# FFN output product: stationary tiles 16 bytes further each, and two of three products with their columns backwards

## The chip, the cores and the metric

The kernel runs on one core of a Trainium2 chip. The metric is the device time of one execution in microseconds. The time before is the median of three runs.

## The reference

Two transformer blocks on one sequence of 256 positions and a width of 2048, all in float32. What bears on the change is the feed-forward part of the first block:

```python
D_FF = -(-8 * D_MODEL // (3 * 256)) * 256          # 5632

def swiglu(x, w_in, w_out):
    g, u = jnp.split(x @ w_in, 2, axis=-1)
    return (jax.nn.silu(g) * u) @ w_out

# in first_block
y = swiglu(x, w_ffn_in[l], w_ffn_out[l])            # [256, 2048] @ [2048, 11264], [256, 5632] @ [5632, 2048]
x = layer_norm(ALPHA * x + y, ln_g[l, 2], ln_b[l, 2])
```

Ahead of it stand a mixer of two attentions and a memory attention; behind it the second block. They are not changed.

## The kernel before

All dense products of the kernel go through one scheme. A weight matrix comes in groups: two tiles of 128 rows and 512 columns (GK = 2, NB = 512), 512 KB, loaded by SyncE into one of four slots of `stage` (L328). ScalarE copies a group into `w_hi` in TensorE's reduced float32 format, fp32r (L1241), and VectorE puts what is left, `stage - w_hi`, into `w_lo` (L1705). The activations are split the same way. A float32 product is then three fp32r products: hi with upper weights, hi with the rest, lo with upper weights. `upper(slot)` and `rest(slot)` give the slot's part of `w_hi` and `w_lo`; from four groups ahead of the second block on, two extra slots (`more_stage`, `more_hi`, `more_lo`) take part for twelve groups.

The queue of TensorE is written out by hand. `weights(kts, hi, lo)` walks the groups of one block of 512 output columns; `group` waits for `lo_done`, then calls `half_group` for both halves r of the 256 rows. A half group is six matmuls into the PSUM bank ACC + r: for each of the two tiles t the three products above, with the activations' 128 x 128 tile as the stationary operand and 512 weight columns as the moving one. Each matmul comes with a weight load of its own. The loop in question is

```python
for k, (x, w) in enumerate(((hi, upper), (hi, rest), (lo, upper))):
    ins = mm(ps[:, ACC + r, 0:n], x[:, kt + t, rows], w(slot)[:, t, 0:n],
             start=first and t == 0 and k == 0, stop=last and t == GK - 1 and k == 2)
```

The feed-forward part works in three parts of 4, 4 and 3 blocks of 512 hidden units (FFN_PARTS). In each, `silu(g) * u` is computed block by block, transposed on TensorE (L732), and written by ScalarE into `ff_h` (L1297) and by VectorE into `ff_l` (L1754), two tiles of 128 x 256 at a time. Then the output product follows: four blocks of 512 columns with 16 (in the last part 12) tiles each, `weights(kts=4 * nf, hi=ff_h, lo=ff_l)`. Its `last_tile_at` waits for the last transposed tiles only ahead of group 2 (nf - 1). Over the three parts these are 44 x 4 x 2 = 352 triples of matmuls.

`ff_h` and `ff_l` are tensors of [128, 16, 256] in fp32r: per partition 16 tiles of 1024 bytes, one behind the other, then those of `ff_l`. Their place is shared in time with others: `more_stage` begins 32 KB behind the start of `ff_h`, which is where `ff_l` ends. A tile `align` of [128, 88] keeps the large tensors at their distance from the start of the memory. Other products use the same line with other activations, above all `x_hl` of [128, 16, 2, 256], whose hi and lo tiles alternate. `heads_block` (L707, L710) is the other way round: weights are stationary, activations move, with 512 and 256 columns in turn. The forget gate's product (L1133) has a stationary operand of 8 columns.

Of the kernel before, what the change touches and what calls it, by code (L numbers as in the profile page):

```python
# [22 lines left out]
F32R = mybir.dt.float32r  # L23
# [5 lines left out]
P = 128  # L29
S = 256  # L30
# [124 lines left out]
def some(value):  # L155

    return not isinstance(value, int) or value > 0


def two_blocks(nc, a, out, per):  # L160

    ctx = ExitStack()
    with ctx:
# [5 lines left out]
        def sem(name):  # L169
            if name not in sems:  # L170
                sems[name] = ctx.enter_context(nc.semaphore("s_" + name))
            return sems[name]
# [46 lines left out]
        def shared(*shapes):  # L219

            with ExitStack() as own:
                return [own.enter_context(nc.sbuf_tensor("b_" + n, s, t)) for n, s, t in shapes]
# [38 lines left out]
            ("kmem_t", [P, H_MEM, S], F32), ("vmem", [P, R, H_MEM * HD], F32))  # L261
        (qmem_t, om_h, om_l) = shared(
            ("qmem_t", [P, H_MEM, S], F32), ("om_h", [P, H_MEM, S], F32R), ("om_l", [P, H_MEM, S], F32R))
        (ff_h, ff_l) = shared(("ff_h", [P, 4 * 4, S], F32R), ("ff_l", [P, 4 * 4, S], F32R))
        (_, more_stage, more_hi, more_lo) = shared(
            ("pad_more", [P, 32 * S], F32), ("more_stage", [P, MORE, GK, NB], F32),
            ("more_hi", [P, MORE, GK, NB], F32R), ("more_lo", [P, MORE, GK, NB], F32R))
# [7 lines left out]
        ps = ctx.enter_context(nc.psum_tensor("b_ps", [P, 8, NB], F32))  # L275
        ACC, TP, SC, AUX, PT, OT = 0, 2, 4, 5, 6, 7
# [359 lines left out]
        def _(pe):  # L636

            c = Counts("pe", per)
            mm, T = nc.tensor.matmul, nc.tensor.transpose

            def group(kt, first, last, hi, lo, n=NB):

                slot, _ = slot_of(c.base.get("g", 0) + c.local.get("g", 0))
                pe.wait_ge(sem("lo_done"), c.next("lo_done"))
                for r in range(R):
                    half_group(slot, r, kt, first, last, hi, lo, n)
                c.next("g")

            def half_group(slot, r, kt, first, last, hi, lo, n=NB):

                if first and some(c.value(f"tile_out{r}")):
                    pe.wait_ge(sem(f"tile_out{r}"), c.value(f"tile_out{r}"))
                for t in range(GK):
                    rows = slice(r * P, (r + 1) * P)
                    for k, (x, w) in enumerate(((hi, upper), (hi, rest), (lo, upper))):
                        ins = mm(ps[:, ACC + r, 0:n], x[:, kt + t, rows], w(slot)[:, t, 0:n],  # L656
                                 start=first and t == 0 and k == 0, stop=last and t == GK - 1 and k == 2)
                if r == 1:
                    ins.then_inc(sem("w_used"), 1)
                elif last:  # L660
                    ins.then_inc(sem("tile0_done"), 1)

            def by_halves(n, kt, first, last, hi, lo, ready=None):

                slots = [slot_of(c.value("g") + i)[0] for i in range(n)]
                for r in range(R):
                    for i in range(n):
                        if ready:
                            ready(r, i)
                        if r == 0:  # L670
                            pe.wait_ge(sem("lo_done"), c.next("lo_done"))
                        half_group(slots[i], r, kt + i * GK, first and i == 0, last and i == n - 1, hi, lo)
                c.next("g", n)
# [410 lines left out]
            for kt in range(2):  # L1084
                pe.wait_ge(sem(f"tile_out{kt}"), c.value(f"tile_out{kt}"))
                for h in range(H_MEM):
                    if kt == 0:
                        pe.wait_ge(sem("pt_ready"), c.next("pt_ready"))
                    ins = mm(mem_out[h], vmem[:, kt, h * HD:(h + 1) * HD],
                             mem_pt[h][:, kt * S:(kt + 1) * S], start=kt == 0, stop=kt == 1)  # L1090
# [1411 lines left out]
def lay_out(nc, shapes, per):  # L2502
    a = {k: nc.dram_tensor("in_" + k, list(s), F32, kind="ExternalInput").ap() for k, s in shapes.items()}
    out = nc.dram_tensor("out", [S, D], F32, kind="ExternalOutput").ap()
    two_blocks(nc, a, out, per)
# [16 lines left out]
```

## Time and profile before

| | |
|---|---|
| median of three runs | 2231.52 us (2231.26 to 2232.51) |
| profiled execution, its own time | 2231.99 us |
| its span | 2230.4 us |
| TensorE busy | 2220.3 us |
| VectorE busy | 1304.6 us |
| ScalarE busy | 1053.9 us |
| GpSimd busy | 178.5 us |
| bytes read | 417.98 MB, 188 GB/s over the span |
| granted TensorE clock | full |

The span reaches from the first to the last instruction of the program; the execution's own time holds 1.6 us more. Busy times count the time in which at least one instruction of the engine is under way. Matmuls overlap each other in the records, so their single durations say little of the rate.

### The profile page before, as it was taken

The numbers are of one execution on the slowest core, as the hardware profiler recorded it, in microseconds if no ns is written. First come the engines' busy times: TensorE is split into PE (matmuls) and PEld (weight loads), VectorE is DVE, ScalarE is ACT, GpSimd is POOL, SyncE is SP. The second block draws the span as 40 slices with busy tenths as digits, with TensorE's granted clock in tenths as the row PEclk, the third lists the DMA queues.
The fourth block names the chain that finished last, engine by engine and source line by source line (L and its number), as shares of the span: only waits on it lengthen the run. The fifth ranks groups of instructions, "written<-read, shape, count | busy, mean of one in ns | idle before, by whom it ended". The sixth has DMA issues, their size and how long they took to land.

```text
span 2230.4 us, 29901 instructions
## 1 busy us (share of the span) xinstructions
PE 2220.3 (100%) x10457; PEld 1850.8 (83%) x10457; DVE 1304.6 (58%) x1589; ACT 1053.9 (47%) x1283; POOL 178.5 (8%) x187
## 2 busy tenths in 40 slices
PE   9999999999999999999999999999999999999999
PEld 8888888888888888888888888888888888888887
DVE  5556655666667754454545445566656655655674
ACT  4444445555444544443444334446445444545643
POOL 1000000001304220000000000003000000200020
PEclk9999999999999999999999999999999999999999
DMA  7755654656856466656665565654566656665554
GB/s 233 230 173 166 191 160 147 192 165 219 263 174 213 134 202 197 202 198 193 191 190 187 191 196 181 197 199 151 170 189 198 206 177 186 207 189 176 167 189 166
DMA packets 216873, 421.33 MB, mean 189 GB/s; under 512 B 15400, under 2 KB 19536, under 8 KB 215120
## 3 DMA queue, kind: packets, MB, share of 16 engines
q1 hardware_dynamic: 212928, 401.79, 57.0%
q0 software_dynamic: 3584, 17.83, 2.4%
q8 instruction: 57, 0.93, 0.2%
q10 hardware_dynamic: 272, 0.52, 0.1%
q14 instruction: 32, 0.26, 0.0%
HBM read 417.98 MB, written 2.11 MB: 188 GB/s over the span
## 4 chain that ended last, share of the span: by engine, by line
PE 98%; POOL 1%; DVE 1%; ACT 0%; DMA 0%; issue 0%; ACTq 0%; DVEq 0%; SPq 0%; POOLq 0%
PE b_ps L656 82%; PE b_ps L707 7%; PE b_ps L710 3%; PE b_ps L749 1%; PE b_ps L832 1%; PE b_ps L732 1%; PE b_ps L847 1%; POOL b_x_res L554 0%; PE b_ps L841 0%; POOL b_x_res L556 0%; PE b_ps L932 0%; PE b_ps L901 0%; PE b_ps L848 0%; DMA b_gate_a<-in_x 0%; DVE b_w_lo L1705 0%; PE b_ps L1133 0%
## 5 line engine op out<-in xcount | busy, mean ns | idle before, releaser
L656 PE MATMUL b_ps<-b_w_hi,b_x_hl 128*128 128x512 f32 (+1 forms) x4144 | 1312.7, 392 | 1.2 <-DVE b_x_hl L1780 1.1
L1705 DVE TENSOR_TENSOR b_w_lo<-b_stage,b_w_hi 128x1024 fp32r<-128x1024 f32 (+1 forms) x756 | 932.8, 1253 | 577.0 <-ACT b_w_hi L1241 573.8
L1241 ACT ACTIVATE b_w_hi<-b_stage 128x1024 fp32r<-128x1024 f32 (+1 forms) x758 | 790.3, 1054 | 677.3 <-PE b_ps L656 590.3
L656 PEld LDWEIGHTS b_ps<-b_w_hi,b_x_hl 128*128 128x128 f32 x4144 | 777.1, 188 | 159.2 <-DVE b_x_hl L1780 1.3
L656 PE MATMUL b_ps<-b_w_lo,b_x_hl 128*128 128x512 f32 (+1 forms) x2072 | 804.4, 388 | 0.0
L656 PEld LDWEIGHTS b_ps<-b_w_lo,b_x_hl 128*128 128x128 f32 x2072 | 389.5, 188 | 76.9
L707 PE MATMUL b_ps<-b_x_hl,b_w_hi 128*128 128x512 f32 x576 | 205.8, 402 | 0.2 <-DVE b_w_lo L1705 0.2
L710 PE MATMUL b_ps<-b_x_hl,b_w_lo 128*128 128x256 f32 x568 | 159.3, 281 | 0.0
L656 PE MATMUL b_ps<-b_w_hi,b_ff_h 128*128 128x512 f32 x344 | 134.1, 390 | 0.0
L656 PE MATMUL b_ps<-b_w_hi,b_ff_l 128*128 128x512 f32 x344 | 133.9, 389 | 0.0
L656 PE MATMUL b_ps<-b_w_lo,b_ff_h 128*128 128x512 f32 x344 | 133.9, 389 | 0.0
L707 PEld LDWEIGHTS b_ps<-b_x_hl,b_w_hi 128*128 128x128 f32 x576 | 108.7, 189 | 28.8 <-issue 3.2
L710 PEld LDWEIGHTS b_ps<-b_x_hl,b_w_lo 128*128 128x128 f32 x568 | 107.3, 189 | 0.0
L656 PEld LDWEIGHTS b_ps<-b_w_hi,b_ff_l 128*128 128x128 f32 x344 | 64.6, 188 | 13.5
L656 PEld LDWEIGHTS b_ps<-b_w_hi,b_ff_h 128*128 128x128 f32 x344 | 64.6, 188 | 13.4
L656 PEld LDWEIGHTS b_ps<-b_w_lo,b_ff_h 128*128 128x128 f32 x344 | 64.6, 188 | 13.2
L554 POOL TENSOR_TENSOR b_x_res<-b_x_res,b_vec_a 128x512 f32<-128x512 f32 x16 | 28.1, 1758 | 568.0 <-ACT b_x_res L1326 557.2
L1857 DVE SCALAR_TENSOR_TENSOR b_x_res<-b_x_res,b_ps 128x512 f32<-128x512 f32 (+1 forms) x48 | 33.0, 687 | 47.6 <-PE b_ps L656 47.1
L1373 ACT ACTIVATE b_logits<-b_logits,b_nmax 128x128 f32<-128x128 f32 (+1 forms) x48 | 21.5, 448 | 79.8 <-DVE b_nmax L1806 79.8
L656 PE MATMUL b_ps<-b_w_hi,b_oh 128*128 128x512 f32 x136 | 53.7, 395 | 0.0
L656 PE MATMUL b_ps<-b_w_hi,b_ol 128*128 128x512 f32 x136 | 53.0, 390 | 0.0
L656 PE MATMUL b_ps<-b_w_lo,b_oh 128*128 128x512 f32 x136 | 53.0, 389 | 0.0
(328 smaller groups left out, 1536.9 us busy)
## 6 DMA issues: line engine op xcount, KB each, us to landing
b_stage<-in_w_in SPq DMA_DIRECT2D x333, 512.0 KB, 4.1
b_stage<-in_w_ffn_in SPq DMA_DIRECT2D x176, 512.0 KB, 4.5
b_stage<-in_w_ffn_out SPq DMA_DIRECT2D x86, 512.0 KB, 4.0
b_stage<-in_w_out SPq DMA_DIRECT2D x64, 512.0 KB, 4.1
b_stage<-in_w_up SPq DMA_DIRECT2D x24, 512.0 KB, 4.0
b_stage<-in_w_o_dsa SPq DMA_DIRECT2D x16, 512.0 KB, 4.5
b_stage<-in_w_o_moba SPq DMA_DIRECT2D x16, 512.0 KB, 4.1
b_stage<-in_w_kv_mem SPq DMA_DIRECT2D x16, 512.0 KB, 3.6
```

The lines of the kernel that those rows point to most:

```text
L554: pool.tensor_tensor(x, x, vec_a[:, cols], ALU.mult).then_inc(sem("pool_step"), 1)
L656: ins = mm(ps[:, ACC + r, 0:n], x[:, kt + t, rows], w(slot)[:, t, 0:n], start=first and t == 0 and k == 0, stop=last and t == GK - 1 and k ...
L707: mm(ps[:, bank, :], upper(slot)[:, t, cols], flat(hl[:, j * GK + t, :, :]), start=j == 0 and t == 0, stop=False)
L710: ins = mm(ps[:, bank, 0:S], rest(slot)[:, t, cols], hl[:, j * GK + t, 0, :], start=False, stop=last and t == GK - 1)
L732: ins = T(ps[:, TP + j // 2, (j % 2) * S + r * P:(j % 2) * S + (r + 1) * P], nat[:, r, j * P:(j + 1) * P], ident[:, :])
L749: ins = T(ps[:, TP + t % 2, kk * S + r * P:kk * S + (r + 1) * P], src[:, r, (2 * t + kk) * P:(2 * t + kk + 1) * P], ident[:, :])
L832: ins = mm(ps[:, SC, lo:hi], q[:, t * P:(t + 1) * P], keys(hi - lo), start=k == 0, stop=k == len(pairs) - 1)
L847: mm(ps[:, bank, col:col + S], v0, probs_t[:, 0:S], start=True, stop=False)
L1241: act.activation(upper(slot)[:, :, 0:n], landing(slot)[:, :, 0:n], ACT.Copy)\
L1373: ins = act.activation(logits[:, 0, lo:hi], logits[:, 0, lo:hi], ACT.Exp, bias=nmax[:, t:t + 1], accum_out=rsum[:, t:t + 1])
L1705: dve.tensor_tensor(rest(slot)[:, :, 0:n], landing(slot)[:, :, 0:n], upper(slot)[:, :, 0:n].bitcast(F32), ALU.subtract).then_inc(sem("lo_d ...
L1857: dve.scalar_tensor_tensor(out=x, in0=x, scalar=alpha, in1=ps[:, ACC + r, :], op0=ALU.mult, op1=ALU.add).then_inc(sem(f"tile_out{r}"), 1)
```

## The change

The rows of `ff_h` and `ff_l` become four elements longer, 260 instead of 256. A tile keeps its 256 elements, and tile k of each tensor starts 16k bytes further than before; `ff_l` as a whole starts 256 bytes further. In the output product the two products with the upper weights (k = 0 and k = 2) read their 512 moving columns from the last to the first and write the result's columns in the same order, so each value lands where it did. The product with the rest of the weights (k = 1) stays forward. All other products are as before.

```diff
-        (ff_h, ff_l) = shared(("ff_h", [P, 4 * 4, S], F32R), ("ff_l", [P, 4 * 4, S], F32R))
+        (ff_rows, fl_rows) = shared(("ff_h", [P, 4 * 4, S + 4], F32R), ("ff_l", [P, 4 * 4, S + 4], F32R))
+        ff_h, ff_l = ff_rows[:, :, 0:S], fl_rows[:, :, 0:S]
@@
                     for k, (x, w) in enumerate(((hi, upper), (hi, rest), (lo, upper))):
-                        ins = mm(ps[:, ACC + r, 0:n], x[:, kt + t, rows], w(slot)[:, t, 0:n],
+                        to, by = ps[:, ACC + r, 0:n], w(slot)[:, t, 0:n]
+                        if hi is ff_h and k != 1:
+                            to, by = to[:, ::-1], by[:, ::-1]
+                        ins = mm(to, x[:, kt + t, rows], by,
                                  start=first and t == 0 and k == 0, stop=last and t == GK - 1 and k == 2)
```

## Rows read from the trace of the kernel before

**Rows 1.** The page: busy us (share of the span) and instructions; the chain by engine and line.
```profile
PE 2220.3 (100%) x10457; PEld 1850.8 (83%) x10457; DVE 1304.6 (58%) x1589; ACT 1053.9 (47%) x1283; POOL 178.5 (8%) x187
...
PE 98%; POOL 1%; DVE 1%; ACT 0%; DMA 0%; issue 0%; ACTq 0%; DVEq 0%; SPq 0%; POOLq 0%
PE b_ps L656 82%; PE b_ps L707 7%; PE b_ps L710 3%; PE b_ps L749 1%; PE b_ps L832 1%; PE b_ps L732 1%; PE b_ps L847 1%; POOL b_x_res L554 0%; PE b_ps L841 0%; POOL b_x_res L556 0%; PE b_ps L932 0%; PE b_ps L901 0%; PE b_ps L848 0%; DMA b_gate_a<-in_x 0%; DVE b_w_lo L1705 0%; PE b_ps L1133 0%
```

**Rows 2.** Busy time by stretch: the one with the output products.
```profile
core 0: us, PE busy (x) PEld busy (x) DVE busy (x) ACT busy (x) POOL busy (x), PEclk, DMA share, GB/s
...
949.00:1502.00 553.00, 553.00 (x2477) 458.56 (x2476) 286.35 (x272) 229.12 (x235) 1.26 (x2) 1.00 0.60 194
```

**Rows 3.** Instructions on the upper weights, by tile: duration ns min/median/max, first and last start.
```profile
L656 PE MATMUL b_ps<-b_w_hi,b_ff_h x344: 389/389/476, 950.0 to 1500.7; 128*128 128x512 f32 x172
...
L656 PE MATMUL b_ps<-b_more_hi,b_ff_h x8: 389/389/390, 1490.5 to 1497.9; 128*128 128x512 f32 x8
```

**Rows 4.** The chain in two output stretches, in order of time: start us, us, what.
```profile
952.92 0.87 PE b_ps L732 x8
953.79 130.58 PE b_ps L656 x576
...
1438.89 62.62 PE b_ps L656 x276
```

**Rows 5.** Timeline, 1000.5 to 1001.5 us: start us, us, engine, line, out<-in.
```profile
1000.57 0.39 PE L656 MATMUL b_ps<-b_w_hi,b_ff_h 128*128 128x512 f32 x1
1000.57 0.19 PEld L656 LDWEIGHTS b_ps<-b_w_lo,b_ff_h 128*128 128x128 f32 x1
1000.79 0.39 PE L656 MATMUL b_ps<-b_w_lo,b_ff_h 128*128 128x512 f32 x1
1000.79 0.19 PEld L656 LDWEIGHTS b_ps<-b_w_hi,b_ff_l 128*128 128x128 f32 x1
1001.02 0.39 PE L656 MATMUL b_ps<-b_w_hi,b_ff_l 128*128 128x512 f32 x1
...
1001.25 0.39 PE L656 MATMUL b_ps<-b_w_hi,b_ff_h 128*128 128x512 f32 x1
```

**Rows 6.** The chain at 36 us: L656 with 336 columns.
```profile
35.81 14.73 PE b_ps L656 x96
```

**Rows 7.** Instructions on ff_h and ff_l, by tile: their writers.
```profile
L1297 ACT ACTIVATE b_ff_h<-b_ps x22: 591/596/599, 820.4 to 1439.2; 128x512 f32 x16, 128x512 fp32r<-128x512 f32 x6
...
L1754 DVE TENSOR_TENSOR b_ff_l<-b_ps,b_ff_h x22: 680/686/692, 821.2 to 1440.0; 128x512 f32 x16, 128x512 fp32r<-128x512 f32 x6
```

**Rows 8.** The chain at the forget gate's product; its weight loads, by tile.
```profile
1530.92 3.21 PE b_ps L1133 x28
...
L1133 PEld LDWEIGHTS b_ps<-b_x_hl,b_wf x32: 87/88/88, 1530.1 to 1533.7; 128*8 128x8 f32 x32
```

**Rows 9.** Timeline of L707 and L710, three pairs at 77 us and three at 84 us.
```profile
77.23 0.40 PE L707 MATMUL b_ps<-b_x_hl,b_w_hi 128*128 128x512 f32 x1
77.46 0.28 PE L710 MATMUL b_ps<-b_x_hl,b_w_lo 128*128 128x256 f32 x1
77.58 0.40 PE L707 MATMUL b_ps<-b_x_hl,b_w_hi 128*128 128x512 f32 x1
77.82 0.28 PE L710 MATMUL b_ps<-b_x_hl,b_w_lo 128*128 128x256 f32 x1
...
78.29 0.40 PE L707 MATMUL b_ps<-b_x_hl,b_w_hi 128*128 128x512 f32 x1
...
83.98 0.39 PE L707 MATMUL b_ps<-b_x_hl,b_w_hi 128*128 128x512 f32 x1
84.21 0.28 PE L710 MATMUL b_ps<-b_x_hl,b_w_lo 128*128 128x256 f32 x1
...
85.02 0.39 PE L707 MATMUL b_ps<-b_x_hl,b_w_hi 128*128 128x512 f32 x1
```

**Rows 10.** The chain at 511 us: plain float32 products, 256 and 128 columns.
```profile
510.82 0.43 PE b_ps L847 x2
511.25 0.22 PE b_ps L848 x2
```

## The prediction

> **What bounds the kernel.** I read the page first: busy time, the forty slices, then the chain that ended last. TensorE is busy for 2220.3 of the 2230.4 us and the chain lies on it for 98% [rows 1]; the line of the change, L656, holds 82% of the chain. The granted clock is full in all slices. Then I cut the span at the products that change. They lie between 949 and 1502 us; in that stretch VectorE works 286 and ScalarE 229 of 553 us, and the DMA engines move 194 GB/s at a share of 0.60 [rows 2]. So in this stretch nothing but TensorE sets the time, and what the change costs or gives per matmul reaches the end of the kernel undiluted.
>
> A matmul's own duration (389 ns, [rows 3]) is useless here, since the matmuls are pipelined: it is the step from one start to the next that counts. The chain gives it best. 576 matmuls of L656 in 130.58 us are 226.7 ns each, and 276 in 62.62 us are 226.9 ns [rows 4]. Three forms of L656 stand in one group of six (w_hi with ff_h, w_lo with ff_h, w_hi with ff_l), and the timeline shows no difference between them: 0.22 or 0.23 us from start to start for all [rows 5].
>
> What is this step made of? The same line with 336 columns takes 14.73 us for 96 matmuls, 153.4 ns [rows 6]. From 336 to 512 columns 73.3 ns are added for 176 columns, which is 0.416 ns a column: one column per cycle of the 2.4 GHz clock. 512 columns are then 213.3 ns, and a pause of 13.4 ns is left at every matmul. Only two things can move: the 0.416 ns, if backward columns run at another rate, and the 13.4 ns, if the position of the stationary tile or the direction of the columns has a part in it.
>
> **The parts of the change.** No instruction is added or removed: the matmuls keep their number, order, banks and semaphores. The counts are 344 + 8 of each of the three forms [rows 3]: 1056 matmuls read a moved stationary tile, and the two forms with the upper weights, 704, run backwards.
>
> *The wider rows of ff_h and ff_l.* ScalarE and VectorE write two tiles at a time with a gap of 16 bytes instead of 512 elements in one piece, 22 times each, 596 and 686 ns [rows 7]. Even 0.1 us more for each of the 44 would be 4.4 us of two engines with some 590 us idle between them over the stretch (553 - 286 and 553 - 229); TensorE asks for the last tiles only after 2(nf - 1) groups, six groups of twelve matmuls or 16 us later in the first two parts. I put it at 0. ff_l now reaches 496 bytes into the first extra staging slot, but only with its sixteenth tile, which the third part (twelve tiles) does not use, and only in the third part is that slot filled. No wait: 0.
>
> *The moved tile as a source of weights.* The weight load takes 188 ns and starts together with the matmul before it [rows 5], so it ends 39 ns ahead of its use. A few nanoseconds more for a shifted start are hidden; were they over 39 ns, they would show in full. What is not hidden is what the load does to the columns that stream beside it. The nearest rows speak on both sides. With stationary tiles of 8 columns, 256 moving columns take 3.21 us for 28, 114.6 ns, so the pause is 114.6 - 106.7 = 8.0 ns [rows 8]: at most 13.4 - 8.0 = 5.4 ns seem to belong to the length of the weight load. And in the head projections, which alternate 512 and 256 columns, the same two lines take 1.06 us for three pairs at 77 us and 1.04 us at 84 us [rows 9], that is 353 against 347 ns a pair, in one and the same block, before and after a few transposes that stand between. Tensors and banks are the same, so I read that difference as one of phase between loads and columns, not of address; single steps there read 0.22 to 0.24 us. So a pause can change with how loads and columns meet, by 3 ns a matmul on the mean and some 10 ns in single ones.
>
> Nothing in the trace shows an operand off its grid: everywhere the step is 226.7 to 226.9 ns, with x_hl, whose tiles stand 2 KB apart, as with ff_h, whose tiles stand 1 KB apart. So I bound the price. Upwards: 10 ns on all 1056 is +10.6 us. Downwards: 5.4 ns on 704 is -3.8 us, on 1056 -5.7 us; the whole pause gone from the 704 backward ones is 704 x 13.4 = -9.4 us, from all 1056 -14.2 us. Nearest is the value that two layouts already share: 0. The Trainium skill, SBUF — State Buffer, "Who interferes with whom", says that TensorE has independent read ports for the moving operand and the weights and waits on nobody. By that rule the term is 0 as well, and both savings above are excluded; the row does not go as far, since it shows a pause without saying what it is.
>
> *The backward columns.* Moving operand and result both run from column 511 to 0, so both are still contiguous. Lower bound of the price: 0 per column. Upper bound: two cycles a column, as the rows with plain float32 operands show (eight 128-column transposes in 0.87 us, 109 ns each, 0.85 ns a column, [rows 4]; two 256-column products in 0.43 us, 0.84 ns a column, [rows 10]). That would be 704 x 213.3 = +150 us. I take 0: a walk of step minus one touches each place once and its neighbour next, as the forward one does, and no row shows a reason for a second cycle.
>
> *The turns.* In a triple the first product ends at result column 0 and the second begins there; the second ends at 511 and the third begins there. Before, each result column rested for a whole matmul between two additions. If an addition still under way held up the next one, it could only do so at the turn, two in each triple, 704 in all. The pause of 13.4 ns already lies between them. Bounds: 0 and, say, a second pause, 704 x 13.4 = +9.4 us. I take 0.
>
> **Sum.** 0 + 0 + 0 + 0. The profiled execution took 1.6 us more than its span, 2231.99 us, and stands 0.5 us above the median of 2231.52. I keep the median: 2231.5 us. What a measurement of this kernel can tell from no change is about 0.2%, 4.5 us, or 6.3 ns on each of the 704 matmuls.
>
> **Rivals.**
>
> *The pause shrinks by more than 0.2% of the time (0.31).* The weight load and the columns hinder each other in the memory they share, and a shifted tile read beside backward columns avoids it. For it: there is a pause at all; it is 5.4 ns shorter with small weights [rows 8]; it varies with phase [rows 9]. Against it: it is the same in x_hl and ff_h, and plain float32 products, whose columns come at half the rate, are not quite comparable. Time: from 2231.5 - 5.7 = 2225.8 to 2231.5 - 9.4 = 2222.1 us, at most 2217.3. It decides from 4.3 ns on all 1056 steps or 6.3 ns on the 704.
>
> *The pause grows by more than 0.2% of the time (0.18).* The tiles leave a grid on which every product of the kernel lies; or the turn waits. Place: the 1056 or the 704 steps of L656 with ff_h and ff_l; price 3 to 13 ns each; +3 to +11 us, up to 2242.5 us. It decides from 4.3 ns on all 1056, or 6.3 ns on 704. For it: the spread of [rows 9] goes upwards from 346.7 ns as easily as down. Against it: it is an effect of order, and the order of L656 has shown one value over thousands of steps.
>
> *The columns at half rate (0.11).* If the result's columns are joined in pairs before they are written, and only upwards, each takes two cycles: 2231.5 + 150 = 2382 us. Against it: the pair of columns lies in the same place either way. The Trainium skill, Advanced Engine Details and Errata, "PSUM Cachelines", says that any non-contiguous pattern slows matmuls significantly, with 8 bytes as the unit; it does not say whether backwards counts as contiguous. No row here shows a backward pattern.
>
> *No effect (0.40)* is the forecast: pause and column rate stay, within 4.5 us either way. Small shifts of the pause (a mean of 1 to 4 ns) belong to it; its own range is 2228 to 2235 us.
>
> **How the numbers follow.** Faster by over 0.2%: the first rival, 0.31. Within 0.2%: 0.40. Slower by over 0.2%: 0.18 + 0.11 = 0.29. The range leaves out the half rate (0.11) and the ends of the other two: from 2221 us, just below the pause gone from the 704, to 2243 us, 10 ns on all 1056 and a little more.
>
> **What would show it.** In the profile after, the chain's long pieces of L656 between 949 and 1502 us give the step: 226.7 ns, and the forecast holds; 213 to 221 ns on the mean, and the pause has shrunk; 230 to 240 ns, and it has grown. The timeline tells which of the three forms it is: a changed step behind the forward form alone points to the load of the moved tile beside forward columns; one at both turns to the result's column; one behind both backward forms to the direction; and a step of 0.44 us to the half rate. A step that differs from tile to tile points to the 16-byte shift. The steps with x_hl must stay at 226.7 ns in any case. The forecast would be wrong if either the position or the direction has a part in the 13.4 ns, which no row separates.

## The result and the profile after

The change makes the kernel slower: 2238.69 us, median of 6 runs (2237.97 to 2241.29), against 2231.61 us for the kernel before in the same comparison. The ratio is 1.0032 with a 95% interval of 1.0022 to 1.0043, or 7.1 us.

L656 of before is L660 now. The page shows the same work, busy for longer:

```profile
PE 2227.1 (100%) x10457; PEld 1850.2 (83%) x10457; DVE 1305.0 (58%) x1589; ACT 1054.4 (47%) x1283; POOL 178.1 (8%) x187
...
PE b_ps L660 82%; PE b_ps L711 7%; PE b_ps L714 3%; PE b_ps L753 1%; PE b_ps L836 1%; PE b_ps L736 1%; PE b_ps L851 1%; POOL b_x_res L555 0%; PE b_ps L845 0%; POOL b_x_res L557 0%; PE b_ps L936 0%; PE b_ps L905 0%; PE b_ps L852 0%; DMA b_gate_a<-in_x 0%; DVE b_w_lo L1709 0%; PE b_ps L1137 0%
```

TensorE is busy for 6.8 us more [rows 1], VectorE and ScalarE for under 1 us more. The chain, in order of time (start us, us, what), has the three output stretches and one stretch that does not touch ff_h:

```profile
216.77 51.69 PE b_ps L660 x228
...
953.34 133.09 PE b_ps L660 x576
...
1220.67 133.09 PE b_ps L660 x576
...
1443.54 64.49 PE b_ps L660 x276
```

The reading of such a piece is used all through what follows. As in the prediction, the step is the time from the start of one matmul to the start of the next, and the pause is what the step has over 512 columns at 0.416 ns. A piece of 576 holds the last 372 matmuls of an output product (31 groups of 12) and the first 204 of the next hidden block (17 groups), which read x_hl. A step with x_hl is 51.69 / 228 = 226.7 ns in both kernels, so these 204 take 46.25 us. The output product's step is (133.09 - 46.25) / 372 = 233.4 ns, where [rows 4] gives (130.58 - 46.25) / 372 = 226.7. The last piece is pure: 64.49 / 276 = 233.7 against 226.9 ns. The surcharge of 6.7 ns on 1056 matmuls is 7.1 us, which is the whole difference. Where an experiment below leaves a part as it was, its piece comes back to within 0.01 us of 130.58 or 62.62 us (e5_read_write, e15_heads_shifted), so even a single run tells steps apart to some 0.1 ns.

All three forms carry it, the forward one (w_lo) too: the median steps behind the three products are 234, 234 and 233 ns, where the kernel before has 227, 226 and 227. The timeline (start us, us, engine, line, out<-in) has steps of 0.23 and 0.24 us where [rows 5] has 0.22 and 0.23:

```profile
1000.11 0.40 PE L660 MATMUL b_ps<-b_w_hi,b_ff_h 128*128 128x512 f32 x1
1000.35 0.40 PE L660 MATMUL b_ps<-b_w_lo,b_ff_h 128*128 128x512 f32 x1
1000.58 0.40 PE L660 MATMUL b_ps<-b_w_hi,b_ff_l 128*128 128x512 f32 x1
1000.82 0.40 PE L660 MATMUL b_ps<-b_w_hi,b_ff_h 128*128 128x512 f32 x1
```

Taken position by position, the median steps lie between 227 and 240 ns. The pattern changes from tile to tile, and in the last three column blocks of a part it repeats within 1 ns (in the first block 9 positions of 10 agree with it). So the steps follow from the program's order of tiles, not from chance. The weight loads still take 188 ns, and the writers of ff_h and ff_l 596 and 686 ns, as in [rows 7].

### The profile page after: what moved, and what is told of

It reads as the page before. It is cut to its first block, busy times and chain, and to the rows that moved or that the text cites. A ratio compares the mean times of both kernels' runs of the same rounds, so it can differ in the third digit from the quotient of the medians.

```text
span 2237.0 us, 29901 instructions
## 1 busy us (share of the span) xinstructions
PE 2227.1 (100%) x10457; PEld 1850.2 (83%) x10457; DVE 1305.0 (58%) x1589; ACT 1054.4 (47%) x1283; POOL 178.1 (8%) x187
## 4 chain that ended last, share of the span: by engine, by line
PE 98%; POOL 1%; DVE 1%; ACT 0%; DMA 0%; issue 0%; ACTq 0%; DVEq 0%; SPq 0%; POOLq 0%
PE b_ps L660 82%; PE b_ps L711 7%; PE b_ps L714 3%; PE b_ps L753 1%; PE b_ps L836 1%; PE b_ps L736 1%; PE b_ps L851 1%; POOL b_x_res L555 0%; PE b_ps L845 0%; POOL b_x_res L557 0%; PE b_ps L936 0%; PE b_ps L905 0%; PE b_ps L852 0%; DMA b_gate_a<-in_x 0%; DVE b_w_lo L1709 0%; PE b_ps L1137 0%
## 5 line engine op out<-in xcount | busy, mean ns | idle before, releaser
L660 PE MATMUL b_ps<-b_w_hi,b_x_hl 128*128 128x512 f32 (+1 forms) x4144 | 1312.5, 392 | 1.2 <-DVE b_x_hl L1784 1.1
L660 PEld LDWEIGHTS b_ps<-b_w_hi,b_x_hl 128*128 128x128 f32 x4144 | 777.0, 188 | 159.7 <-DVE b_x_hl L1784 1.3
L660 PE MATMUL b_ps<-b_w_lo,b_x_hl 128*128 128x512 f32 (+1 forms) x2072 | 804.3, 388 | 0.0
L660 PEld LDWEIGHTS b_ps<-b_w_lo,b_x_hl 128*128 128x128 f32 x2072 | 389.5, 188 | 76.8
L660 PE MATMUL b_ps<-b_w_hi,b_ff_h 128*128 128x512 f32 x344 | 137.0, 398 | 0.0
L660 PE MATMUL b_ps<-b_w_hi,b_ff_l 128*128 128x512 f32 x344 | 136.3, 396 | 0.0
L660 PE MATMUL b_ps<-b_w_lo,b_ff_h 128*128 128x512 f32 x344 | 136.0, 395 | 0.0
L660 PEld LDWEIGHTS b_ps<-b_w_hi,b_ff_l 128*128 128x128 f32 x344 | 64.7, 188 | 15.9
L660 PEld LDWEIGHTS b_ps<-b_w_lo,b_ff_h 128*128 128x128 f32 x344 | 64.7, 188 | 15.5
L660 PEld LDWEIGHTS b_ps<-b_w_hi,b_ff_h 128*128 128x128 f32 x344 | 64.6, 188 | 15.4
L660 PE MATMUL b_ps<-b_w_hi,b_oh 128*128 128x512 f32 x136 | 53.7, 395 | 0.0
L660 PE MATMUL b_ps<-b_w_hi,b_ol 128*128 128x512 f32 x136 | 53.0, 390 | 0.0
L660 PE MATMUL b_ps<-b_w_lo,b_oh 128*128 128x512 f32 x136 | 52.9, 389 | 0.0
```

The source lines that it names most:

```text
L660: ins = mm(to, x[:, kt + t, rows], by, start=first and t == 0 and k == 0, stop=last and t == GK - 1 and k == 2)
```

## The experiments

The theories at the start: *position* (the stationary tile off its grid), *direction* (the backward columns), *turn* (the result's columns touched twice in succession), *joint* (position and direction are each free alone).

**The two halves of the change.** `e1_rows` has the longer rows, all forward; `e2_back` the short rows and k = 0 and 2 backward.

```diff
 # e1_rows, against the changed kernel
-                        if hi is ff_h and k != 1:
-                            to, by = to[:, ::-1], by[:, ::-1]
 # e2_back, against the changed kernel
-        ... ("ff_h", [P, 4 * 4, S + 4], F32R), ("ff_l", [P, 4 * 4, S + 4], F32R))
+        ... ("ff_h", [P, 4 * 4, S + 0], F32R), ("ff_l", [P, 4 * 4, S + 0], F32R))
```

> The longer rows of ff_h and ff_l alone, all columns forward. Position theory (a stationary tile off the common grid costs a longer pause whatever the direction): the step of the output products is 233 to 234 ns as after the change, the time 2238 to 2239 us. Direction theory (the backward columns cost it): 226.7 ns, 2231.6 us. Joint theory (each is free alone): 226.7 ns as well, and the next kernel tells it from the direction theory.

Measured: 2236.93 us, ratio 1.0024 (1.0014 to 1.0033). The chain of this kernel:

```profile
955.00 132.63 PE b_ps L658 x576
...
1444.19 63.86 PE b_ps L658 x276
```

(132.63 - 46.25) / 372 = 232.2 ns. The longer rows alone cost some three quarters of the surcharge.

> The backward columns of the two products with upper weights alone, all tiles on their old places. Position theory: 226.7 ns a step, 2231.6 us. Direction theory: about 233.5 ns on the mean, 2238.7 us; if the result's column at the turn is what waits, the steps behind the first and the second product of a triple are long and the one behind the third is 226.7 ns. Joint theory: 226.7 ns, 2231.6 us.

Measured: 2239.08 us, ratio 1.0033 (1.0021 to 1.0046). The chain:

```profile
953.09 133.05 PE b_ps L660 x576
...
1443.18 64.42 PE b_ps L660 x276
```

(133.05 - 46.25) / 372 = 233.3 ns. The backward columns alone cost as much as both together. So each half costs, and the two do not add up: position, direction and joint theory are each wrong as the single cause. The order inside a triple is now the same for every tile: median steps of 240, 229 and 231 ns, 700 in all. In each the long step is the one behind k = 0. The turn theory had asked for 226.7 behind k = 2; it has 231.

**All three backward**, with short and with long rows.

```diff
-                        if hi is ff_h and k != 1:
+                        if hi is ff_h and k in (0, 1, 2):
```

> All three products backward, tiles on their old places, so that no turn is left. Position theory: 226.7 ns. Direction theory: 1056 instead of 704 steps are long, up to 237 ns a step on the mean, 2242 us. Turn theory: 226.7 ns, since there are no turns.

> The longer rows with all three products backward. Position theory: 233 to 234 ns a step, about 2238.7 us, as with two backward. Direction theory: more than with two backward, some 2242 us. Turn theory: 226.7 ns, 2231.6 us.

Measured: 2239.09 and 2239.19 us in one run each. The chains of e3_back_all, then of e4_rows_back_all:

```profile
953.97 133.07 PE b_ps L660 x576
```

```profile
953.06 133.41 PE b_ps L660 x576
```

These are 233.4 and 234.3 ns. With the old rows three backward products cost no more than two, against the direction theory's sum; with the longer rows they cost 1 ns more. With no turn left the surcharge stays, against the turn theory.

**Read or write.** Part 1 only reads backward, part 2 only writes backward (the result is mirrored in both), part 3 is as before. From here on the three parts of the output product are set apart, each with its own tensors for ff_h and ff_l, in the same place of the memory, and its own flags. Such a kernel's time mixes three parts, so the step of each part is read instead; the times were 2233.24 to 2238.55 us, one run each, but for `e9_both_shifted`, where the whole kernel is touched.

```diff
+                        to, by = ps[:, ACC + r, 0:n], w(slot)[:, t, 0:n]
+                        if hi is ff_h and k in back:
+                            to = to if mode == "read" else to[:, ::-1]
+                            by = by if mode == "write" else by[:, ::-1]
```

> Tiles on their old places. Part 1 of the output products reads its moving columns backward in all three products and writes the result forward; part 2 reads forward and writes the result backward; part 3 is as before. The result's columns therefore stand mirrored in parts 1 and 2. Collision theory (the moving read and the weight load hinder each other in the memory of the operands): part 1 has 233.3 ns a step, part 2 226.7. Result theory (writing backward costs it): part 1 226.7, part 2 233.3 ns. Part 3: 226.7 in either case.

The chain of this kernel, parts 1, 2 and 3:

```profile
953.75 133.07 PE b_ps L669 x576
...
1221.01 130.58 PE b_ps L669 x576
...
1441.36 62.62 PE b_ps L669 x276
```

233.4, 226.7 and 226.9 ns: it is the read. Writing 512 result columns backward costs nothing that can be seen. A backward read also begins elsewhere, at column 511, which is 4 bytes short of a multiple of 256 from where the forward one begins. No run here reads backward from a moved start, so the direction and the place where the read begins are not told apart.

**Where the tile may start.** All forward; ff_h and ff_l moved as a whole.

```diff
 # (start of ff_h, start of ff_l, row length) in elements, by part; e6_shift_16_32_64
+        FF = {0: (4, 4, 256, ...), 4: (8, 8, 256, ...), 8: (16, 16, 256, ...)}
 # e7_shift_128_256_48
+        FF = {0: (32, 32, 256, ...), 4: (64, 64, 256, ...), 8: (12, 12, 256, ...)}
```

> All columns forward. All tiles of ff_h and ff_l together are moved by 16 bytes in part 1, 32 bytes in part 2 and 64 bytes in part 3. Off-grid theory (any start off the common grid costs the same): one step near 232 ns in all three parts. Collision theory (what counts is which line of a small pattern a load meets, so each distance has a cost of its own): different steps, constant within a part, some perhaps at 226.7 ns or below, and their mean near the 232.0 ns of the longer rows.

> As the kernel before it, with 128, 256 and 48 bytes. Collision theory: from some power of two on the pattern repeats and the step is 226.7 ns again, first at 256 bytes, perhaps already at 128; 48 bytes has a step of its own. Off-grid theory: 48 bytes costs 232 ns, 128 and 256 bytes whatever the grid is.

The chain with 16, 32 and 64 bytes:

```profile
953.08 133.06 PE b_ps L669 x576
...
1220.40 133.06 PE b_ps L669 x576
...
1443.24 64.42 PE b_ps L669 x276
```

The chain with 128, 256 and 48 bytes:

```profile
953.77 132.72 PE b_ps L669 x576
...
1220.66 130.58 PE b_ps L669 x576
...
1441.05 64.41 PE b_ps L669 x276
```

16, 32, 48 and 64 bytes all give 233.4 ns, 128 bytes 232.4, and 256 bytes 226.7. Of these shifts only 256 bytes is free, and the grid is called one of 256 bytes from here on. The traces hold no addresses: a place on the grid means a whole multiple of 256 bytes from where the tile stood before. My collision theory had expected a price for each distance; the off-grid theory, one price for all, was nearly right. It does not explain e1_rows tile by tile. There tile k lies 16k bytes further, so tile 0 is on the grid and tile 8 is off by 128 bytes; an estimate from the shifts above is (226.7 + 232.4 + 14 x 233.4) / 16 = 232.9 ns, and 232.2 was measured. But tile 0 has 232.8 ns on the mean in the first two parts, and the cheapest are tiles 5 and 11, with 228.6 and 229.8. So a tile's price depends on its neighbours in the queue too.

**Backward with other starts.**

> All three products backward, tiles moved by 16, 32 and 64 bytes in parts 1, 2 and 3. Collision theory: backward needs another place, so one of these may reach 226.7 ns or less, against 233.3 ns on the old places. Off-grid theory with a price of its own for the direction: never under 233.3 ns.

> All three products backward, tiles moved by 128, 192 and 240 bytes in parts 1, 2 and 3. If the backward read only needs another distance, one of these may lock at 226.7 ns; if a backward read never locks, all three have 233.3 ns, as the distances 0, 16, 32 and 64 had.

```diff
 # e8_back_16_32_64 (and with 32, 48 and 60 elements e12_back_128_192_240)
+        FF = {0: (4, 4, 256, (0, 1, 2), ''), 4: (8, 8, 256, (0, 1, 2), ''), 8: (16, 16, 256, (0, 1, 2), '')}
```

The longest pieces of part 1 in the one and the other:

```profile
953.00 133.09 PE b_ps L669 x576
```

```profile
953.26 133.10 PE b_ps L669 x576
```

All six starts give 233.4 to 233.5 ns. No place of the stationary tile that I tried makes three backward reads cheap.

**Both operands moved.** w_hi and w_lo start 16 bytes later in the whole kernel (they stand in one new tensor behind `v_st`, and `x_hl` moves into their old place); ff_h and ff_l 16, 0 and 32 bytes in parts 1, 2 and 3.

> All columns forward. The moving operand, w_hi and w_lo, is moved by 16 bytes in the whole kernel; the tiles of ff_h and ff_l by 16 bytes in part 1, not at all in part 2, by 32 bytes in part 3. Distance theory (what counts is the distance between the stationary tile and the moving columns, modulo 256 bytes): part 1 has 226.7 ns a step, parts 2 and 3 have 233.3, and all products with x_hl go to 233.3 ns, so that the kernel takes 40 to 55 us more. Place theory (each operand must start on a multiple of 256 bytes): 233.3 ns in part 1 and with x_hl. If only the stationary tile's place counts: part 2 and x_hl stay at 226.7 ns.

```diff
+        w_flat = sb("w_hi_lo", [P, 2 * SLOTS * GK * NB + 8], F32R)
+        w_hi, w_lo = [w_flat[:, 4 + k * SLOTS * GK * NB:4 + (k + 1) * SLOTS * GK * NB].rearrange(
+            "p (s t n) -> p s t n", s=SLOTS, t=GK) for k in range(2)]
```

2263.67 us in one run. The chain, a stretch with 336 columns, one of x_hl alone, and parts 1, 2 and 3:

```profile
35.04 14.72 PE b_ps L670 x96
...
915.25 44.49 PE b_ps L670 x192
...
960.62 133.24 PE b_ps L670 x576
...
1230.79 133.44 PE b_ps L670 x576
...
1455.76 65.17 PE b_ps L670 x276
```

x_hl has 44.49 / 192 = 231.7 ns here, and with that taken off the pieces part 1 has 231.1 and part 2 231.6 ns; part 3 has 65.17 / 276 = 236.1 ns, the dearest of all runs. The distance theory fails, since an equal shift of both does not bring 226.7 back. The place theory is right in kind, not in size: moving columns off the grid cost 5 ns and not 6.7, with the stationary tiles 16 bytes off it is no more, and with 32 bytes it is 9.4. The kernel is 31.6 us slower than the one before, where the distance theory had 40 to 55. The 336-column product is as before (153.3 against 153.4 ns, [rows 6]), which neither theory said.

**One tensor, and less than a line.**

> All columns forward. Part 1: only ff_l moved by 16 bytes; part 2: only ff_h; part 3: both by 4 bytes. Local theory (each load pays for itself): part 1 one step of three is 20 ns/3 longer, mean 228.9 ns; part 2 two of three, mean 231.1 ns. Lock theory (one load out of place throws the others out too): 233.3 ns mean in both. 4 bytes: 233.3 ns if the distance must be zero to the byte, 226.7 ns if only the line of 16 bytes counts.

Only ff_l moved, only ff_h moved, both moved by 4 bytes (one element). The chain:

```profile
954.13 132.65 PE b_ps L669 x576
...
1220.96 133.06 PE b_ps L669 x576
...
1443.82 64.24 PE b_ps L669 x276
```

232.3, 233.4 and 232.8 ns. With only one load of three out of place, the mean is nearly as high as with all: the local theory (228.9) fails, the lock theory is close. Four bytes are enough.

**One or two backward reads.** e11_one_back reads and writes k = 1 backward in part 1 and k = 0 in part 2; in part 3, k = 0 and 2 write backward and read forward. e14_pairs_back has k = 0 and 1, then k = 1 and 2, and in part 3 a shift of 8 bytes.

> Tiles on their old places. Part 1: only the product with the rest of the weights (k = 1) backward; part 2: only the first product (k = 0); part 3: k = 0 and 2 write backward but read forward, so that the result's columns turn twice in a triple while the read never does (the result is mirrored there for two of three products). Local theory: 228.9 ns mean in parts 1 and 2. Lock theory: 233.3 ns. Turn theory, already weak: over 226.7 ns in part 3; without it 226.7.

The chain:

```profile
953.41 131.41 PE b_ps L669 x576
...
1219.00 131.43 PE b_ps L669 x576
...
1440.17 62.62 PE b_ps L669 x276
```

228.9, 229.0 and 226.9 ns. One backward read pays for itself alone: the timeline of part 1 has the step behind w_lo at 0.24 us and the other two at 0.22 and 0.22 to 0.23 (medians 227, 233, 227 ns).

```profile
999.96 0.39 PE L669 MATMUL b_ps<-b_w_hi,b_ff_h 128*128 128x512 f32 x1
1000.18 0.40 PE L669 MATMUL b_ps<-b_w_lo,b_ff_h 128*128 128x512 f32 x1
1000.42 0.39 PE L669 MATMUL b_ps<-b_w_hi,b_ff_l 128*128 128x512 f32 x1
1000.64 0.39 PE L669 MATMUL b_ps<-b_w_hi,b_ff_h 128*128 128x512 f32 x1
```

Part 3 ends the turn theory: the result turns twice in each triple and the step stays at that of before.

> Tiles on their places. Part 1: k = 0 and 1 backward, part 2: k = 1 and 2. Each neighbour pair theory (one backward read costs 6.7 ns in its own step, and a step next to another backward one costs more): 20 ns a triple in both parts, 233.3 ns mean, as with 0 and 2. If every backward read simply costs its own 6.7 ns: 231.1 ns mean. Part 3: forward, both tensors moved by 8 bytes, that is inside a line of 16 bytes: like 4 bytes, near 232 ns with some steps at 226.7, or like 16 bytes, 233.3 ns.

The chain:

```profile
952.82 133.09 PE b_ps L669 x576
...
1220.13 133.09 PE b_ps L669 x576
...
1442.99 63.68 PE b_ps L669 x276
```

Both pairs give 233.4 ns; the median steps are 231, 240, 229 with k = 0 and 1 backward and 229, 231, 240 with k = 1 and 2. With k = 0 and 2 they were 240, 229, 231. The long step is always that of the second backward read of a pair (k = 2 and the next k = 0 are neighbours as well). So a triple costs 680 ns without, 687 with one, 700 with two or three backward reads. The 8 bytes give 230.7 ns.

**A load half as long.** The stationary tile has 64 columns, so half of the result's rows are left out. Part 1 forward on the grid, part 2 all backward, part 3 forward and moved by 16 bytes.

> The stationary tile of the output products has 64 instead of 128 columns, so half of each half's rows are left out of the product and the load beside the moving columns is half as long. Part 1: forward, on the grid. Part 2: all three backward, on the grid. Part 3: forward, moved by 16 bytes. Collision theory (moving reads and weight load hinder each other while both run): the surcharge of parts 2 and 3 over part 1 shrinks with the load, to about 3.3 ns, and the pause of part 1 is under 13.4 ns, about 10. Theory of a fixed price (a backward or off-grid operand costs some start-up of its own): the surcharge stays at 6.7 ns.

```diff
+                        if hi is ff_h and wide < P:
+                            rows, to = slice(r * P, r * P + wide), to[0:wide]
```

The chain, and a weight load by tile (ns min/median/max):

```profile
952.96 131.82 PE b_ps L671 x576
...
1219.03 133.06 PE b_ps L671 x576
...
1441.87 64.41 PE b_ps L671 x276
...
L671 PEld LDWEIGHTS b_ps<-b_w_hi,b_ff_h x344: 133/135/137, 949.0 to 1505.2; 128*64 128x64 f32 x172
```

The load is shorter, 135 for 188 ns, and nothing gets cheaper: 230.0, 233.4 and 233.4 ns. Part 1 is even dearer than with a full load, with median steps from 224 to 236 ns in a pattern of six. Parts 2 and 3 lie 3.4 ns over part 1, which is the collision theory's figure, but only because part 1 rose; the theory had it fall. A collision whose price grows with the load's length is out.

**The other way round: off the grid on purpose.** In e9_both_shifted the head projections, whose stationary operand is w_hi and w_lo and whose moving columns alternate between 512 and 256, were faster than before. e15_heads_shifted moves w_hi and w_lo by 16 bytes for these 72 groups alone. To make room, both tensors stand behind `v_st` as a whole, and `x_hl` and the tensors after it move up by 32 KB.

```diff
+        w_hi, w_lo, early_hi, early_lo = (w_ring(n, at) for at in (0, 4) for n in ("w_hi", "w_lo"))
@@ (in slot_of)
+    if isinstance(g, int) and g < 9 * KT // GK:
+        return Early(g % SLOTS), SLOTS        # upper() and rest() take early_hi and early_lo for it
```

> The kernel before, with w_hi and w_lo moved by 16 bytes for the first 72 groups only, those of the head projections, where these are the stationary operand and 512 and 256 moving columns alternate. The kernel with w_hi and w_lo moved throughout had 347 ns a pair there in place of mostly 353. Theory that the off-grid stationary tile keeps the alternating products in their cheaper rhythm: the 504 pairs of L707 and L710 fall to 347 ns each, 2 to 3 us less in all, 2229 us, ratio 0.999. If that rhythm came from something else that the other kernel changed: no change, 2231.6 us.

Measured: 2229.22 us, median of 11 runs, against 2231.52; ratio 0.9990 (0.9981 to 0.9999). The timeline at the place of [rows 9] (three pairs in 1.04 us where they took 1.06), and the chain at the product with 336 columns, 35.81 us in the kernel before, and where the heads are done, 217.31 us there:

```profile
77.48 0.39 PE L721 MATMUL b_ps<-b_x_hl,b_w_hi 128*128 128x512 f32 x1
77.71 0.28 PE L724 MATMUL b_ps<-b_x_hl,b_w_lo 128*128 128x256 f32 x1
...
78.52 0.39 PE L721 MATMUL b_ps<-b_x_hl,b_w_hi 128*128 128x512 f32 x1
...
35.18 14.72 PE b_ps L670 x96
...
214.46 51.69 PE b_ps L670 x228
```

It reaches that point 2.9 us earlier; 0.6 us of this is there at the first of the two pieces, whose start differs by up to 1 us between the kernels of this study, and 2.2 us are gained between them. The median is 2.3 us lower.

Is it the 16 bytes or the new place of the tensors? A later block, on the memory's keys, runs the same two lines, and there this kernel has w_hi and w_lo in the new place but not shifted. Its three pairs take 1.06 us, as in the kernel before; in e9_both_shifted, which is shifted there too, they take 1.04. This kernel, then e9_both_shifted:

```profile
660.45 0.40 PE L721 MATMUL b_ps<-b_mem_hl,b_w_hi 128*128 128x512 f32 x1
...
661.51 0.40 PE L721 MATMUL b_ps<-b_mem_hl,b_w_hi 128*128 128x512 f32 x1
```

```profile
666.76 0.39 PE L721 MATMUL b_ps<-b_mem_hl,b_w_hi_lo 128*128 128x512 f32 x1
...
667.80 0.39 PE L721 MATMUL b_ps<-b_mem_hl,b_w_hi_lo 128*128 128x512 f32 x1
```

So it is the 16 bytes. The unshifted products of L670 with x_hl keep their step as well (43.57 us for 192), so the new place is not what slowed them in e9_both_shifted. This is the fastest version of the study, faster than both kernels by a margin that the interval just clears.

## Why the prediction was wrong

The forecast was no effect: 2231.5 us, with at most 4.5 us either way. The kernel came out 7.1 us slower. That lies inside the stated range only because the range took in a rival, the pause that grows.

- **TensorE sets the time there, and a cost per matmul arrives undiluted.** Right: 1056 x 6.7 ns = 7.1 us, and 7.1 us were measured.
- **The wider rows cost the writers nothing.** Right: 596 and 686 ns as before, and no new wait.
- **The moved tile as a source of weights: 0.** Wrong; this is one of the two terms that failed. It costs 5.5 ns a step alone in the first two parts of e1_rows and 4.5 in the third, which is 5.5 us by the chain's pieces and 5.3 us by the medians. I took the value on which x_hl and ff_h agree. But both, 2 KB and 1 KB apart, lie on the same grid of 256 bytes, so their agreement said nothing of a tile off it. The text even named this ("nothing in the trace shows an operand off its grid") and then chose 0 as the nearest row. The row to weigh was [rows 9], where a pair takes 353 or 347 ns with nothing moved: it told that pauses in such a stream can change by some nanoseconds. That it is the same effect is not shown.
- **The Trainium skill, SBUF — State Buffer, "Who interferes with whom"**, would have this term at 0, as TensorE's two reads are independent and wait on nobody. The runs do not bear that out as a rule for the time: the place of the stationary tile alone moves the step from 226.7 to 233.4 ns (e6_shift_16_32_64). They do not show that the two reads block each other either; half the load did not halve the price.
- **The row with the small weights.** From [rows 8] the prediction read that up to 5.4 ns of the pause belong to the length of the weight load. With a load 53 ns shorter the pause grew, from 13.4 to 16.7 ns (e13_narrow_loads, part 1), so this reading is not borne out, and with it the savings of 3.8 and 5.7 us.
- **The backward columns: 0 per column.** Right as to the rate and the result's side: there is no half rate, and writing backward is free. At half rate, as in the prediction's rival, the step would be 2 x 213.3 + 13.4 = 440 ns, and it is 226.7 ns in e5_read_write, part 2. The Trainium skill, Advanced Engine Details and Errata, "PSUM Cachelines", says that non-contiguous patterns slow matmuls significantly; by this run a contiguous run of columns written backward is not among them. Wrong as to the read, the second term that failed: it lengthens the pause from 13.4 to 20.0 ns on the mean.
- **The turns: 0.** Right, shown by e5_read_write and by part 3 of e11_one_back.
- **The sum.** Two terms of 0 should have been 5.5 and 6.6 ns on 1056 steps, each alone. They do not add: together they gave 6.7 ns. Why they do not is open; 233.4 ns is no ceiling, since e4_rows_back_all has 234.3 and part 3 of e9_both_shifted 236.1. The rival "the pause grows" was right in place and size (3 to 13 ns on 1056 steps) and had 0.18. Of its signs, steps that differ from tile to tile came with the moved tiles; the backward columns made one long step in a triple, behind k = 0 (e2_back), and not one behind each backward product.

What is shown: each half of the change costs by itself; the price lies on the operands' reads and not on the result; the forward, on-grid stream has 226.7 ns, and every other arrangement of the reads that was tried, but for 256 bytes, has 228.9 to 236.1. What stays open is the mechanism, and whether a backward read costs for its direction or for where it begins. Neither the distance between the operands, nor the length of the load, nor a price per operand explains all runs: two backward reads cost as much as three, one shifted tensor nearly as much as two, and products of 336 columns take no harm from moving columns off the grid (their stationary tiles were never moved). A rhythm between load and columns, in which one operand out of step spoils its neighbours, fits these, but it was not measured by itself.

## What to carry to other kernels

For a stream of fp32r products of 512 columns, keep both the stationary tiles and the moving rows whole multiples of 256 bytes apart, as here, and read forward: pad rows by 256 bytes or a multiple, not by a few elements. When layouts agree in a trace, ask what they have in common before taking their value for one that leaves it. Where the stream alternates 512 and 256 columns the same grid was the dearer place, so the step from start to start decides, and it is read from the chain's long pieces.

## What was not expected of the hardware

- The step of a product with 512 columns is 226.7 ns (a pause of 13.4) with both operands on the grid of 256 bytes and read forward, and 233.3 to 233.4 ns (20.0) with the stationary tiles 16 to 64 bytes off it. 4 bytes off already give 232.8 ns.
- Reading moving columns backward costs 6.7 ns for one product of three and 20 ns for two or three; writing the result backward costs nothing.
- A stationary tile of 64 columns makes the step longer, 230.0 ns, not shorter, though its load takes 53 ns less.
- Moving w_hi and w_lo by 16 bytes makes the alternating products of the heads take 347 ns a pair throughout, where the kernel before has 353 in most stretches and 347 from 84 us on for some 35 us.
